# The heads' inverse root in the first mixer as exp of a logarithm on ScalarE, and two weight splits moved ahead of it

## The chip, the cores and the metric

One core of a Trainium2 chip runs the whole program in one launch. The metric is the device time of that launch in microseconds; lower is better. The engines are TensorE (PE, matrix products), VectorE (DVE), ScalarE (ACT), GpSimd (POOL) and SyncE (SP), which here only issues the loads of weights.

## What is computed

The reference runs two transformer blocks in float32 over 512 tokens of width 1024. The change lies in the first block's mixer:

```python
def l2_normalize(x):
    x32 = x.astype(jnp.float32)
    return x32 * lax.rsqrt(jnp.sum(x32 * x32, axis=-1, keepdims=True) + L2_EPS)

def hybrid_mixer(h, w_in, conv_qkv_w, ...):
    p = h @ w_in
    qkv = jax.nn.silu(causal_depthwise_conv(p[..., Q_OFF:Z_OFF], conv_qkv_w))
    q, k, v = ...                                   # 4 heads of 128 each
    o = gated_delta_rule_chunked(l2_normalize(q), l2_normalize(k), v, g, beta)
    ...
```

Four heads of k and four of q, each 128 x 512 (channels on partitions, tokens along the row), are divided by the root of their sum of squares plus 1e-6; q is also scaled by 128^-0.5. Behind the mixer come its output product, a feed-forward, and then the second block (feed-forward, a mixer with attention and a second recurrence, feed-forward, norm). None of that is touched.

## The kernel before

Everything is written out by hand: each engine has its own function (`tensor`, `vector`, `scalar`, `gpsimd`, `sync`), runs its instructions in the order in which they stand there, and waits on counting semaphores. `X.at(i)` is the point a waiter waits for, `X.up(i)` the increment.

**Weights.** They come as slabs of 128 x 1024 float32, one for each tile of 128 output columns. SyncE loads them into a ring of four buffers `RAWS` (L2270), strictly in the order of the list `ORDER`. In the stretch of the change that list alternates: a slab of `w_in`, then a slab of `ada`, and so on. A load waits until its buffer, used four entries earlier, has been read. For a `w_in` slab that means the split of the one two before it; for an `ada` slab, VectorE's weighing (`ada(j)`, L1024) of the one two before it. Each `w_in` slab is split into an upper part WH and a lower part WL, three buffers of each: ScalarE copies WH (L1625, `split_to`, reached through `begin(which, j, ahead)`), and GpSimd subtracts (L2087). A slab's WH waits for the product that used the same buffer three slabs earlier. The product itself (L490, `slab_gemm`) waits for WL and runs three passes over eight k tiles, 24 matmuls of 128 x 512.

**The mixer's first part.** `IN_ORDER` is the order of the `w_in` tiles: four heads of k, four of q, four of v (index i = 0 to 11), then four z tiles and twelve of the short convolution. I call the weights of index i "slab i" and its product "product i". The products write two PSUM banks in turn (`main_bank`), so product i waits until the result two places before it in the list `MAIN` has been copied out. `MAIN` has the `ada` column 2 between product 9 and product 10, so product 10 waits for tile 9, product 11 for VectorE's `modulation(2)` and product 12 for tile 10.

For each of the tiles 0 to 11, ScalarE's `convolve(i)` copies the product from PSUM to a staging buffer `STG` (L1702, `cv_ev`); VectorE's `convolve(i)` forms the causal convolution of width 4 with one TENSOR_SCALAR (L1106) and three SCALAR_TENSOR_TENSOR (L1109); ScalarE applies silu (L1704) and, for the eight tiles of k and q, squares the result into `L2S[i]` (L1707), which lies in `X`. In each turn i of its loop ScalarE first splits slab i + 1, and then calls `convolve(i - 1)`; VectorE first weighs an `ada` slab and then convolves. From i = 10 on, both go on in `project_rest`, a generator that is interleaved with the delta rule's generators by a fixed number of ticks.

**The heads' norm.** It runs in two batches of four tiles. TensorE sums the squares over the partitions with a matrix of ones (`l2_sums`, L554), after product 5 and after the `ada` column 2. ScalarE takes the roots from PSUM (`l2_roots`, L1712), in the turn i = 6 behind `convolve(5)`, and behind `convolve(9)`. VectorE divides (`unit_heads`): a RECIPROCAL (L1116) and one SCALAR_TENSOR_TENSOR (L1118) for each tile, in the turn i = 7 behind `convolve(6)`, and behind `convolve(9)` and `modulation(2)`.

**Function tables.** The compiler puts an ACT_TABLE_LOAD before a function that the loaded set does not have. `log_and_exp()` (L1632) is an explicit load of the set that has Ln and Exp; one also stands before `project_rest` starts, behind the second batch. Copy and Square cause no load in the profile.

The delta rule's `prepare` begins during product 13: TensorE (L662), then VectorE (L1255) and ScalarE (L1803), and waits for the end of the heads' norm.

Of the kernel before, what the change touches and what calls it, by code (L numbers as in the profile page):

```python
# [40 lines left out]
IN_ORDER = [4, 5, 6, 7, 0, 1, 2, 3] + list(range(8, 28))  # L41
# [105 lines left out]
def program(nc, xT, metaT, cols, consts, slabs, lup, gup, out):  # L147
    f32, f32r = mybir.dt.float32, mybir.dt.float32r
    ALU, ACT = mybir.AluOpType, mybir.ActivationFunctionType
    ve, ae, ge, te, se = nc.vector, nc.scalar, nc.gpsimd, nc.tensor, nc.sync  # L150
# [5 lines left out]
    def steps(name, *names):  # L156
        return Steps(sem(name), *names)

    def count(name):
        return Count(sem(name))  # L160
# [10 lines left out]
    def bank(i):  # L171
        return PS[:, i, :]
# [19 lines left out]
    EPSC = sbuf("EPSC", [128, 1])  # L192
# [144 lines left out]
    z_ev, sc_ev = count("z_ev"), count("sc_ev")  # L337
    sc = steps("sc", "prod", "t0", "t1", "t2", "y")
    cat1_hi, cat1_lo = count("cat1_hi"), count("cat1_lo")
    l2_sq, l2_mm, l2_rt = count("l2_sq"), count("l2_mm"), count("l2_rt")  # L340
    l2 = steps("l2", "rec", "mul")


    INV_PE = ("i1", "i2", "i3", "i4", "i5", "i6", "i7", "i8", "i9a", "i9b", "i10", "i11a", "i11b", "i12")
# [87 lines left out]
    L2S = [XF[:, 512 * i:512 * i + 512] for i in range(8)]  # L432
# [45 lines left out]
    def tensor():  # L478
# [70 lines left out]
        def l2_sums(i0):  # L549
            for i in range(i0, i0 + 4):  # L550
                if i in (4, 5):
                    te.wait_ge(*l2_rt.at(i - 2))
                te.wait_ge(*l2_sq.at(i))
                te.matmul(bank(i if i0 else 2 + i), con("ones"), L2S[i], start=True, stop=True).then_inc(*l2_mm.up(i))  # L554

# [93 lines left out]
        def prepare(b):  # L649
            e, t = b % 2, b // 2  # L650
            p, d, a = pp[e], dp[e], ap[e]
            A, B = bank(2 + 2 * e), bank(3 + 2 * e)
            ts = slice(128 * b, 128 * b + 128)
            te.wait_ge(s_k1, 32)
            te.wait_ge(*row_c.at("colt"))
            if t:
                te.wait_ge(*d.at("w2", t - 1))
                te.wait_ge(*a.at("w1", t - 1))
            else:
                te.wait_ge(*l2_rt.at(5 if e else 1))  # L660
            for h in range(4):
                ins = te.matmul(A[:, 128 * h:128 * h + 128], con("sel", 64)[:, 128 * h:128 * h + 128], ROW[:, ts],  # L662
                                start=True, stop=True)
            ins.then_inc(*p.up("g", t))
            for h in range(4):
                ins = te.matmul(B[:, 128 * h:128 * h + 128], con("sel", 64)[:, 128 * (4 + h):128 * (4 + h) + 128],
                                ROW[:, ts], start=True, stop=True)
            ins.then_inc(*p.up("bb", t))
            yield
            yield  # L670
            yield
            te.wait_ge(*a.at("eg", t))
            te.wait_ge(*l2.at("mul", 7))
            te.wait_ge(*d.at("kb", t))
            for h in range(4):
                for c, q in enumerate(HALF):
                    t0 = 64 * (2 * b + c)
                    te.matmul(A[q, 64 * h:64 * h + 64], QKV[:, 4 + h, t0:t0 + 64], KB[e][:, h, 64 * c:64 * c + 64],
                              start=True, stop=True)
                    ins = te.matmul(B[q, 64 * h:64 * h + 64], QKV[:, 4 + h, t0:t0 + 64], QKV[:, h, t0:t0 + 64],  # L680
                                    start=True, stop=True)
            ins.then_inc(*p.up("kq", t))
            yield
            te.wait_ge(*cv_si.at(11))
            te.wait_ge(*d.at("at", t))
            for h in range(4):
                te.transpose(A[:, 128 * h:128 * h + 128], QKV[:, 4 + h, ts], con("ident"))
                ins = te.transpose(B[:, 128 * h:128 * h + 128], QKV[:, 8 + h, ts], con("ident"))
            ins.then_inc(*p.up("tr", t))
            yield  # L690
            te.wait_ge(*d.at("vbt", t))
            yield from invert(inv[e], UU[e], p, d, a, gp[e], t, A, B)
            te.wait_ge(*d.at("x", t))
            for h in range(4):
                for q in HALF:
                    ins = te.matmul(A[q, 128 * h:128 * h + 128], XX[e][q, h, :], VBT[e][q, h, :], start=True, stop=True)
            ins.then_inc(*p.up("u", t))
            yield
            te.wait_ge(*a.at("u", t))
            for h in range(4):  # L700
                for q, o in zip(HALF, (B, A)):
                    ins = te.matmul(o[:, 64 * h:64 * h + 64], KBT[e][q, h, :], XX[e][q, h, :], start=True, stop=True)
            ins.then_inc(*p.up("w", t))

        def scan(b):
            e, t = b % 2, b // 2
            for c, q in enumerate(HALF):
                n = 2 * b + c
                te.wait_ge(*dp[e].at("w2", t))
                te.wait_ge(*ap[e].at("w1", t))  # L710
                if n:
                    te.wait_ge(*sd.at("st3", n - 1))
                    te.wait_ge(*so.at(n - 1))
                    if c == 0:
                        te.wait_ge(*gt_r.at("ln", b - 1))
                else:
                    te.wait_ge(*zeros.at("st"))
                    te.wait_ge(*l2_rt.at(7))
                for h in range(4):
                    ins = te.matmul(PS[q, 6, 128 * h:128 * h + 128], WT[e][:, 4 * c + h, :], ST[:, h, :], start=True,  # L720
                                    stop=True)
                ins.then_inc(*sp.up("s", n))
                yield
                te.wait_ge(*sd.at("vn", n))
                for h in range(4):
                    ins = te.matmul(PS[:, 7, 128 * h:128 * h + 128], KDT[e][q, h, :], VN[q, h, :], start=True, stop=True)
                ins.then_inc(*sp.up("sd", n))

                for h in range(4):
                    te.matmul(PS[:, 6, 64 * h:64 * h + 64], ST[:, h, :], QD[e][:, h, 64 * c:64 * c + 64], start=h == 0,  # L730
                              stop=False, skip_group_check=True)
                for h in range(4):
                    ins = te.matmul(PS[:, 6, 64 * h:64 * h + 64], VN[q, h, :], AT[e][q, h, :], start=False, stop=True,
                                    skip_group_check=True)
                ins.then_inc(*sp.up("o", n))
                yield
            te.wait_ge(*gt_sq.at(b))
            te.matmul(bank(6), con("ones"), RSTD[:, 0:512], start=True, stop=True).then_inc(*gt_mm.up(b))
            yield
            yield  # L740
# [272 lines left out]
    def vector():  # L1013
# [98 lines left out]
        def unit_heads(i0):  # L1112
            for i in range(i0, i0 + 4):
                j = IN_ORDER[i]
                ve.wait_ge(*l2_rt.at(i))
                ve.reciprocal(L2S[i], L2S[i]).then_inc(*l2.up("rec", i))  # L1116
                ve.wait_ge(*l2.at("rec", i))
                ve.scalar_tensor_tensor(QKV[:, j, :], QKV[:, j, :], 128.0 ** -0.5 if j < 4 else 1.0, L2S[i], ALU.mult,  # L1118
                                        ALU.mult).then_inc(*l2.up("mul", i))

        for i in range(1, 10):
            ada(i + 15)
# [118 lines left out]
        def prepare(b):  # L1241
            e, t = b % 2, b // 2
# [16 lines left out]
            ve.wait_ge(*d.at("dc1", t))  # L1259
            ve.tensor_tensor(dv, dv, over(con("madd"), 4), ALU.add).then_inc(*d.up("dm", t))  # L1260
            ve.wait_ge(*p.at("bb", t))
            ve.wait_ge(*l2.at("mul", 7))
            ve.tensor_tensor(KB[e][:, :, :], QKV[:, 4:8, ts], h4(B), ALU.mult).then_inc(*d.up("kb", t))
            ve.wait_ge(*a.at("eg", t))
            ve.tensor_tensor(QD[e][:, :, :], QKV[:, 0:4, ts], EG[e][:, :, :], ALU.mult).then_inc(*d.up("qd", t))
# [348 lines left out]
    def scalar():  # L1614
# [13 lines left out]
        def begin(which, j, ahead=2, cap=len(CUTS)):  # L1628
            split_to(min(CUT[which, j] + ahead, cap))

        def log_and_exp():
            ae.preload_act_table_set("natural_log_exp_and_others")  # L1632
# [74 lines left out]
                ae.activation(L2S[i], QKV[:, j, :], ACT.Square).then_inc(*l2_sq.up(i))  # L1707

        def l2_roots(i0):
            for i in range(i0, i0 + 4):  # L1710
                ae.wait_ge(*l2_mm.at(i))
                ae.activation(L2S[i], bank(i if i0 else 2 + i), ACT.Sqrt, bias=EPSC[:, 0:1]).then_inc(*l2_rt.up(i))  # L1712

        begin("w_in", IN_ORDER[0], 1)
        for i in range(1, 10):
# [14 lines left out]
            if i == 4:  # L1730
                ae.wait_ge(*row_c.at("colt"))
                ae.activation(EGC[:, :, :], COLT[:, :, 0:4], ACT.Exp).then_inc(*row_e.up(0))
            elif i == 6:
                l2_roots(0)
        begin("w_in", IN_ORDER[10], 1)
        convolve(9)
        l2_roots(4)

        def project_rest():
# [52 lines left out]
        def prepare(b):  # L1792
            e, t = b % 2, b // 2
# [5 lines left out]
            if t:  # L1799
                ae.wait_ge(*d.at("qd", t - 1))  # L1800
            else:
                ae.wait_ge(*l2.at("mul", 7))
            ae.activation(EG[e][:, :, :], h4(A), ACT.Exp).then_inc(*a.up("eg", t))  # L1803
            yield
            ae.wait_ge(*d.at("dm", t))
# [650 lines left out]
```

## Time and profile before

| | |
|---|---|
| time, median of 3 runs | 2199.66 us (2195.71 to 2201.82) |
| the profiled execution | 2196.09 us |
| its span, first to last instruction | 2194.9 us |
| PE busy | 1995.6 us, 91% |
| DVE busy | 823.5 us, 38% |
| POOL busy | 760.0 us, 35% |
| ACT busy | 701.4 us, 32% |
| mean granted TensorE clock | 0.957 of full |

The shares are means over the whole span. The change touches only about 75 us of it, from 110 to 185 us after the start, so that stretch has to be read by itself, in the order of time. A row of the timeline has the start, the time until the end of the last instruction of the row, the engine, the line, the operation, the output and inputs, and in brackets how long the engine had been idle before it, and what ended that.

### The profile page before, as it was taken

Reading aid. Unit: us, or ns where it says so; the run is one execution under the profiler, and the core shown is the slowest. Engines: PE = TensorE matmul, PEld = TensorE weight load, DVE = VectorE, ACT = ScalarE, POOL = GpSimd, SP = SyncE. Lnnn points to the kernel's source line nnn. Section 1 sums busy time; section 2 is a strip of 40 time slices with the busy share of each in tenths; the row PEclk is TensorE's granted clock in tenths of the full one; section 3 lists DMA queues with packets and bytes.
Section 4 is the critical chain, followed back from the end, with each engine's and each line's share of the span. In section 5 each row is a group of like instructions: output and inputs, shape, how many; then the busy total and the mean of one; then the engine's idle time right before and its main releaser. Section 6 shows DMA issues by size and latency. Waiting matters only on the chain. (4 is left out here: it accounts for less than half of the span.)

```text
span 2194.9 us, 32154 instructions
## 1 busy us (share of the span) xinstructions
PE 1995.6 (91%) x13960; PEld 1677.6 (76%) x13960; DVE 823.5 (38%) x1073; ACT 701.4 (32%) x1048; POOL 760.0 (35%) x444
## 2 busy tenths in 40 slices
PE   3866998899999999999999888888999789999997
PEld 2645776778888889999999877876676567888885
DVE  6677363332211112443400366654444433444201
ACT  2442221232222323222222333344454324222222
POOL 2312121334444555443344432211011144444453
PEclk9978999899999999999999999899998899999999
DMA  7322221223432232322323412100000232333331
GB/s 268 116 77 96 78 83 63 78 67 135 144 95 89 85 102 91 97 87 87 92 90 90 136 61 73 29 6 2 1 2 2 87 106 81 93 96 96 91 95 64
DMA packets 55659, 182.76 MB, mean 83 GB/s; under 512 B 7488, under 2 KB 7744, under 8 KB 55392
## 3 DMA queue, kind: packets, MB, share of 16 engines
q1 hardware_dynamic: 55520, 180.72, 25.6%
q8 instruction: 110, 1.80, 0.4%
q14 instruction: 29, 0.24, 0.0%
HBM read 175.45 MB, written 5.24 MB: 82 GB/s over the span
## 5 line engine op out<-in xcount | busy, mean ns | idle before, releaser
L2087 POOL TENSOR_TENSOR WL<-RAWS,WH 128x1024 fp32r<-128x1024 f32 (+2 forms) x275 | 647.7, 2358 | 1011.2 <-ACT WH L1625 1011.2
L490 PE MATMUL PS<-HH,WH 128*128 128x264 f32 (+2 forms) x2184 | 673.6, 350 | 58.5 <-issue 31.3
L490 PE MATMUL PS<-HL,WH 128*128 128x264 f32 (+2 forms) x2184 | 657.1, 343 | 0.0
L490 PE MATMUL PS<-HH,WL 128*128 128x264 f32 (+2 forms) x2184 | 654.5, 341 | 0.0
L490 PEld LDWEIGHTS PS<-HH,WH 128*128 128x128 f32 (+1 forms) x2184 | 381.0, 192 | 126.4 <-issue 55.9
L1625 ACT ACTIVATE WH<-RAWS 128x1024 fp32r<-128x1024 f32 (+2 forms) x275 | 283.8, 1033 | 452.7 <-PE PS L490 401.9
L490 PEld LDWEIGHTS PS<-HL,WH 128*128 128x128 f32 (+1 forms) x2184 | 381.2, 191 | 47.7 <-issue 1.9
L490 PEld LDWEIGHTS PS<-HH,WL 128*128 128x128 f32 (+1 forms) x2184 | 380.2, 191 | 48.5 <-issue 0.4
L490 PE MATMUL PS<-IHf,WH 128*128 128x512 f32 (+1 forms) x704 | 209.4, 338 | 0.0
L490 PE MATMUL PS<-IHf,WL 128*128 128x512 f32 (+1 forms) x704 | 209.3, 338 | 0.0
L490 PE MATMUL PS<-ILf,WH 128*128 128x512 f32 (+1 forms) x704 | 209.2, 338 | 0.0
L1372 DVE TENSOR_TENSOR TMP<-TMP,PS 128x512 f32<-128x512 f32 (+1 forms) x66 | 45.8, 693 | 250.9 <-PE PS L490 238.3
L1886 ACT ACTIVATE IHf<-TMP 128x512 fp32r<-128x512 f32 (+1 forms) x66 | 42.0, 636 | 283.4 <-DVE TMP L1372 283.4
L490 PEld LDWEIGHTS PS<-ILf,WH 128*128 128x128 f32 x704 | 120.6, 188 | 14.8
L490 PEld LDWEIGHTS PS<-IHf,WH 128*128 128x128 f32 x704 | 120.5, 188 | 14.8
L490 PEld LDWEIGHTS PS<-IHf,WL 128*128 128x128 f32 x704 | 120.4, 188 | 14.9
L1367 DVE TENSOR_TENSOR TMP<-TMP,RSTD 128x528 f32<-128x528 f32 (+1 forms) x44 | 104.5, 2374 | 41.4 <-ACT TMP L1882 41.4
L1379 DVE SCALAR_TENSOR_TENSOR X<-PS,X 128x528 f32<-128x528 f32 (+1 forms) x16 | 11.2, 699 | 222.5 <-PE PS L490 222.5
L1360 DVE TENSOR_TENSOR TMP<-PS,RSTD 128x528 f32<-128x528 f32 (+1 forms) x44 | 30.8, 700 | 150.9 <-PE PS L490 150.1
L2103 POOL TENSOR_TENSOR SQA<-SQA,TMP 128x512 f32<-128x512 f32 (+1 forms) x39 | 53.1, 1360 | 89.8 <-ACT TMP L1638 89.0
L1374 DVE TENSOR_TENSOR ILf<-TMP,IHf 128x512 fp32r<-128x512 f32 (+1 forms) x66 | 48.8, 740 | 46.4 <-ACT IHf L1886 46.4
L1638 ACT ACTIVATE TMP<-X 128x512 f32<-128x512 f32 (+1 forms) x42 | 26.1, 627 | 85.0 <-DVE X L1379 35.7
(494 smaller groups left out, 1948.8 us busy)
## 6 DMA issues: line engine op xcount, KB each, us to landing
RAWS<-w_w_in SPq DMA_DIRECT2D x52, 512.0 KB, 4.3
RAWS<-w_ada SPq DMA_DIRECT2D x32, 512.0 KB, 3.6
RAWS<-w_f0g SPq DMA_DIRECT2D x22, 512.0 KB, 3.6
RAWS<-w_f0u SPq DMA_DIRECT2D x22, 512.0 KB, 3.7
RAWS<-w_f1g SPq DMA_DIRECT2D x22, 512.0 KB, 3.6
RAWS<-w_f1u SPq DMA_DIRECT2D x22, 512.0 KB, 3.6
RAWS<-w_f2g SPq DMA_DIRECT2D x22, 512.0 KB, 3.6
RAWS<-w_f2u SPq DMA_DIRECT2D x22, 512.0 KB, 3.6
```

The costliest lines, as they stand in the source:

```text
L490: ins = te.matmul(ps[0:m, q, o:o + b - a] if len(halves) > 1 else ps[0:m, o:o + b - a], w[:, k * m:k * m + m], v[:, k0 + k, a:b], start=fi ...
L1360: ve.tensor_tensor(tv, place(f, 2 * j), r, ALU.mult).then_inc(*ff_g.up("g", FT * (f - 1) + j))
L1367: ve.tensor_tensor(tv, tv, r, ALU.mult).then_inc(*ff_g.up("r", FT * (f - 1) + j))
L1372: ve.tensor_tensor(tv, tv, place(f, 2 * j + 1), ALU.mult).then_inc(*ff_mul.up(FT * f + j))
L1374: ve.tensor_tensor(IL[f][:, j, :], t, IH[f][:, j, :].bitcast(f32), ALU.subtract).then_inc(*ff_lo.up(FT * f + j))
L1379: ve.scalar_tensor_tensor(xv, place(f, 2 * FT + m), 0.5 if f else MOD[:, 40 + m:41 + m], xv, ALU.mult, ALU.add).then_inc(*ff_x.up(8 * f + m))
L1625: ae.activation(WH[s % NS][:, 0:n], RAW[i % NR][:, 0:n], ACT.Copy).then_inc(*w_hi.up(s))
L1638: ae.activation((TMP[k % 3] if k else SQA)[:, 0:n], X[:, k, t0:T2], ACT.Square).then_inc(*n_sq.up(8 * SQUARED[q] + k))
L1886: ae.activation(IH[f][:, j, :], t, ACT.Copy).then_inc(*ff_hi.up(FT * f + j))
L2087: ge.tensor_tensor(WL[s % NS][:, 0:n], RAW[i % NR][:, 0:n], WH[s % NS][:, 0:n].bitcast(f32), ALU.subtract).then_inc(*w_lo.up(s))
L2103: ge.tensor_tensor(SQA[:, 0:n], SQA[:, 0:n], TMP[k % 3][:, 0:n], ALU.add).then_inc(*n_acc.up(added(q, k)[1] - 1))
```

## The change

`unit_heads` loses its RECIPROCAL: the SCALAR_TENSOR_TENSOR alone is left, and multiplies by what ScalarE hands over. `l2_roots` becomes a preload of the set with Ln and Exp, four times Ln (bias 1e-6) from PSUM, and four times Exp with scale -0.5 in place, in the place of four times Sqrt. TensorE's waits on `l2_rt`, which guard the PSUM banks, become waits on the new count `l2_ln`.

ScalarE also splits slab 8 before the first batch of roots (it was split behind it, ahead of `convolve(6)`), and slab 12 before the second batch (it was split behind `convolve(10)`'s silu, in `project_rest`). The later calls of `begin` for the same slabs then have nothing left to do. GpSimd's order and SyncE's are not changed.

```diff
@@ tensor()
-                    te.wait_ge(*l2_rt.at(i - 2))
+                    te.wait_ge(*l2_ln.at(i - 2))
@@ vector(), unit_heads
                 ve.wait_ge(*l2_rt.at(i))
-                ve.reciprocal(L2S[i], L2S[i]).then_inc(*l2.up("rec", i))
-                ve.wait_ge(*l2.at("rec", i))
                 ve.scalar_tensor_tensor(QKV[:, j, :], QKV[:, j, :], 128.0 ** -0.5 if j < 4 else 1.0, L2S[i], ALU.mult,
-                                        ALU.mult).then_inc(*l2.up("mul", i))
+                                        ALU.mult).then_inc(*l2.up(i))
@@ scalar()
         def l2_roots(i0):
+            log_and_exp()
             for i in range(i0, i0 + 4):
                 ae.wait_ge(*l2_mm.at(i))
-                ae.activation(L2S[i], bank(i if i0 else 2 + i), ACT.Sqrt, bias=EPSC[:, 0:1]).then_inc(*l2_rt.up(i))
+                ae.activation(L2S[i], bank(i if i0 else 2 + i), ACT.Ln, bias=EPSC[:, 0:1]).then_inc(*l2_ln.up(i))
+            for i in range(i0, i0 + 4):
+                ae.wait_ge(*l2_ln.at(i))
+                ae.activation(L2S[i], L2S[i], ACT.Exp, scale=-0.5).then_inc(*l2_rt.up(i))
@@
             elif i == 6:
+                begin("w_in", IN_ORDER[7], 1)
                 l2_roots(0)
         begin("w_in", IN_ORDER[10], 1)
         convolve(9)
+        begin("w_in", IN_ORDER[11], 1)
         l2_roots(4)
```

## Rows read from the trace of the kernel before

**Rows 1.** What TensorE waited for, 100 to 192 us (total, times, longest).

```profile
PE PS L490 <- issue: 24.2, 3, 17.6
PE PS L525 <- ACT STG L1702: 14.1, 1, 14.1
```

**Rows 2.** Timeline of ScalarE, the first batch and around it.

```profile
103.25 0.63 ACT L1707 ACTIVATE X<-QKV 128x512 f32<-128x512 f32 x1
103.79 1.05 ACT L1625 ACTIVATE WH<-RAWS 128x1024 fp32r<-128x1024 f32 x1
...
110.62 0.63 ACT L1707 ACTIVATE X<-QKV 128x512 f32<-128x512 f32 x1
111.27 1.28 ACT L1712 ACT_TABLE_LOAD   x1
112.57 2.42 ACT L1712 ACTIVATE X<-PS,EPSC 128x512 f32<-128x512 f32 x4
114.86 1.07 ACT L1625 ACTIVATE WH<-RAWS 128x1024 fp32r<-128x1024 f32 x1
115.81 0.61 ACT L1702 ACTIVATE STG<-PS 128x512 f32<-128x512 f32 x1
```

**Rows 3.** Timeline of ScalarE: explicit loads, Ln and Exp in the delta rule and later.

```profile
238.72 1.28 ACT L1632 ACT_TABLE_LOAD   x1
...
458.32 1.28 ACT L1632 ACT_TABLE_LOAD   x1
459.62 0.69 ACT L1653 ACTIVATE RSTD<-PS,EPSC 128x512 f32<-128x512 f32 x1
460.34 0.63 ACT L1655 ACTIVATE RSTD<-RSTD 128x512 f32<-128x512 f32 x1
```

**Rows 4.** Timeline of VectorE, 68 to 140 us.

```profile
68.75 0.49 DVE L1106 TENSOR_SCALAR TMP<-STG,CV 128x512 f32<-128x512 f32 x1
69.28 2.33 DVE L1109 SCALAR_TENSOR_TENSOR TMP<-STG,CV,TMP 128x512 f32<-128x512 f32 x3
71.52 1.28 DVE L1024 SCALAR_TENSOR_TENSOR ACC<-RAWS,CA,ACC 128x1024 f32<-128x1024 f32 x1
...
116.45 2.18 DVE L1106 TENSOR_SCALAR TMP<-STG,CV 128x512 f32<-128x512 f32 x1 [5.33 <-ACT STG L1702]
...
120.91 3.34 DVE L1116 RECIPROCAL X<-X 128x512 f32<-128x512 f32 x1
...
138.18 1.28 DVE L1024 SCALAR_TENSOR_TENSOR ACC<-RAWS,CA,ACC 128x1024 f32<-128x1024 f32 x1
```

**Rows 5.** VectorE's multiply by its line (duration in ns, min/median/max).

```profile
L1118 DVE SCALAR_TENSOR_TENSOR QKV<-QKV,X x8: 691/694/2003, 124.3 to 175.4; 128x512 f32<-128x512 f32 x8
```

**Rows 6.** Timeline of GpSimd: the split of slab 8.

```profile
116.01 2.34 POOL L2087 TENSOR_TENSOR WL<-RAWS,WH 128x1024 fp32r<-128x1024 f32 x1 [8.73 <-ACT WH L1625]
```

**Rows 7.** Timeline of SyncE's queue: the load of slab 10.

```profile
139.86 0.43 SPq L2270 DMA_DIRECT2D RAWS<-w_w_in  x1
```

**Rows 8.** Timeline of ScalarE, between the batches and behind the second.

```profile
144.50 1.06 ACT L1625 ACTIVATE WH<-RAWS 128x1024 fp32r<-128x1024 f32 x1 [0.96 <-DMA RAWS<-w_w_in]
...
157.33 0.63 ACT L1704 ACTIVATE QKV<-TMP 128x512 f32<-128x512 f32 x1 [4.62 <-DVE TMP L1109]
...
180.03 0.63 ACT L1704 ACTIVATE QKV<-TMP 128x512 f32<-128x512 f32 x1 [15.12 <-DVE TMP L1109]
```

**Rows 9.** Timeline of TensorE: the first matmuls of products 12 and 13.

```profile
184.13 0.76 PE L490 MATMUL PS<-HH,WH 128*128 128x512 f32 x1 [17.61 <-issue]
184.69 0.63 PE L490 MATMUL PS<-HL,WH 128*128 128x512 f32 x1
...
191.54 0.40 PE L490 MATMUL PS<-HH,WH 128*128 128x512 f32 x1
```

**Rows 10.** Windows: busy time of PE, PEld, DVE, ACT and POOL, then TensorE's clock.

```profile
112.00:184.00 72.00, 35.14 (x126) 25.84 (x124) 59.06 (x43) 22.80 (x31) 11.74 (x5) 0.74 0.23 79
460.00:850.00 390.00, 386.49 (x1704) 313.63 (x1705) 69.67 (x93) 120.24 (x155) 178.71 (x83) 0.99 0.32 101
```

More of the change, by code:

```diff
@@ L339, in program @@
     cat1_hi, cat1_lo = count("cat1_hi"), count("cat1_lo")
-    l2_sq, l2_mm, l2_rt = count("l2_sq"), count("l2_mm"), count("l2_rt")
-    l2 = steps("l2", "rec", "mul")
+    l2_sq, l2_mm, l2_ln, l2_rt, l2 = (count(x) for x in ("l2_sq", "l2_mm", "l2_ln", "l2_rt", "l2"))
     INV_PE = ("i1", "i2", "i3", "i4", "i5", "i6", "i7", "i8", "i9a", "i9b", "i10", "i11a", "i11b", "i12")
@@ L659, in prepare @@
             else:
-                te.wait_ge(*l2_rt.at(5 if e else 1))
+                te.wait_ge(*l2_ln.at(5 if e else 1))
             for h in range(4):
@@ L672, in prepare @@
             te.wait_ge(*a.at("eg", t))
-            te.wait_ge(*l2.at("mul", 7))
+            te.wait_ge(*l2.at(7))
             te.wait_ge(*d.at("kb", t))
@@ L717, in scan @@
                     te.wait_ge(*zeros.at("st"))
-                    te.wait_ge(*l2_rt.at(7))
+                    te.wait_ge(*l2_ln.at(7))
                 for h in range(4):
@@ L1261, in prepare @@
             ve.wait_ge(*p.at("bb", t))
-            ve.wait_ge(*l2.at("mul", 7))
+            ve.wait_ge(*l2.at(7))
             ve.tensor_tensor(KB[e][:, :, :], QKV[:, 4:8, ts], h4(B), ALU.mult).then_inc(*d.up("kb", t))
@@ L1801, in prepare @@
             else:
-                ae.wait_ge(*l2.at("mul", 7))
+                ae.wait_ge(*l2.at(7))
             ae.activation(EG[e][:, :, :], h4(A), ACT.Exp).then_inc(*a.up("eg", t))
```

## The prediction

> **What bounds the kernel now.** I first read what TensorE waited for, because the change sits in a short stretch and the shares over the whole span say nothing of it. From 100 to 192 us TensorE waits 24.2 us in three pieces put down to "issue" (the longest 17.6) and 14.1 us for a copy to STG [rows 1]. Those 38.3 us of idle time are all that can be won here. Then I read the timelines of ScalarE and VectorE beside each other. In the first batch ScalarE's roots take 3.6 us, and VectorE then spends 17.27 us from the first RECIPROCAL at 120.91 to the next `ada` at 138.18 [rows 2, 4], in pairs of 3.34 and 0.69 us [rows 4, 5]. Everything behind that is held up in turn: silu(7), the split of slab 10, the copy of tile 8 right behind it, for which TensorE waits 14.1 us [rows 1, 8]. In the second batch, silu(9) starts at 157.33 and silu(10) only at 180.03, after 15.12 us of waiting for VectorE [rows 8]; slab 12 is split behind it, and product 12 starts at 184.13 after 17.61 us of idleness [rows 9]. So the bound in this stretch is the chain from VectorE over ScalarE's silu and split to GpSimd's WL, and TensorE is the waiting engine. In 112 to 184 us it is busy 35.14 of 72 us, against 386.49 of 390 in the first feed-forward [rows 10].
>
> **The sum, first batch.** All times are in the profiled execution; nothing changes before ScalarE's square at 110.62 [rows 2].
> - Split of slab 8, moved ahead: an instruction behind a 0.63 us activation starts 0.54 us after it (103.25 to 103.79), so the split runs from 111.16 to 112.23 [rows 2]. Its buffer was loaded and its WH buffer is free, as product 6 is done. GpSimd has WL at about 115.7 in place of 118.35 [rows 6].
> - Load, Ln, Exp: the load starts at 112.23 and the first Ln 1.30 us later [rows 3], at 113.53. I cost four Ln as the four Sqrt, which have the same operands and length (0.69 us), 2.29 us [rows 2, 3]: 115.82. Four Exp from SBUF take 0.63 us each [rows 3], 0.54 us apart: 117.98. If they went at Ln's pace it would be 0.15 us more for a batch. The copy of tile 6 thus starts at 117.98 in place of 115.81, 2.17 us later. Product 8 then waits for this copy (118.6) instead of for WL (118.35): 0.2 us.
> - VectorE's convolution of tile 6 starts at 118.62. GpSimd is idle by then, and TENSOR_SCALAR takes 0.53 us to the next start, as at 68.75, and not 2.18, as at 116.45 beside GpSimd's split [rows 4, 6]. With three SCALAR_TENSOR_TENSOR at 2.24 us together it ends at 121.39, against 120.91. The moved split so pays back most of ScalarE's 2.17 us.
> - The norm on VectorE: four multiplies at 0.69 us each, about 0.61 us apart: 2.44 us in place of 17.27. It ends at 123.83, against 138.18.
> - Next, ScalarE: silu(6) 121.5, square 122.2, split of slab 9 from 122.7, and GpSimd 1.15 us after it (114.86 to 116.01) [rows 2, 6], at 123.86. That is a dead heat with `ada(23)` on VectorE at 123.83. If GpSimd is first, `ada(23)` ends at about 127.1 and the convolution of tile 7 at 129.9. If VectorE is first, `ada(23)` ends at 125.1, GpSimd at 127.5, the TENSOR_SCALAR is held until then, and the convolution ends at 130.0. A multiply of 2.00 us among seven of 0.69 shows this kind of hold on VectorE [rows 5].
> - Slab 10: its load is queued on SyncE behind an `ada` load that waits for `ada(23)`. Before, `ada(23)` ended at 139.46, the load was issued at 139.86, and the split began at 144.50, 5.04 us after `ada(23)` [rows 4, 7, 8]. Now that gives 130.15 or 132.15, and ScalarE is ready at 131.2. The split begins at 131.2 or 132.15: 13.3 or 12.35 us earlier. I take 12.8.
>
> The Trainium skill (SBUF — State Buffer, section "SBUF: two separate sides") states the port shared by VectorE and GpSimd as an exclusive lock: whichever starts first has it for its whole instruction. The row of 2.00 us agrees for GpSimd first; the other case has no row here. By that rule alone either end of the last step is possible, so it speaks for 12.35 as much as for 13.3.
>
> **The sum, second batch.** From slab 10 to silu(9) nothing is changed: 144.50 to 157.33 becomes 131.7 to 144.5 [rows 8]. The split of slab 12 follows at 145.05 (its load waits for `ada(25)`, at about 139, and so lands at about 144), the table load at 146.1, Ln at 147.4, Exp at 149.7. The sums of squares are ready well before. VectorE multiplies from 150.35, each Exp just ahead of it, until 152.8; `ada(26)` to 154.0. ScalarE has one more explicit load, the one that stands ahead of `project_rest`. Though redundant now, it is issued: the row at 458.32 is such a load, and no other set was loaded since the one at 238.72 [rows 3]. So the copy of tile 10 runs from 153.15 to 153.75, hidden behind `ada(26)`; without that cover the 1.3 us would be on the chain. The convolution of tile 10, with no GpSimd beside it, ends at 156.8, and silu(10) starts at 156.9 in place of 180.03: 23.1 us earlier. Then come `ada(27)` and the convolution of tile 11, again unhindered, to 160.85, silu(11) at 160.95, the split of slab 13 at 161.5, and GpSimd from 162.65 to 165.0. Product 12 has its weights long before (slab 12 is moved ahead) and runs at about 154 to 160, right behind product 11. **Product 13** starts at 165.05 in place of 191.54: 26.5 us earlier. But now it is the cold one, after 5 us of idleness. Product 12 took 7.41 us for 24 matmuls after its gap, with 0.76 and 0.63 us rows where later ones have 0.40 [rows 9]; in the feed-forward one comes every 0.229 us, 5.5 us for 24 [rows 10]. So 1.9 us go back. What remains is 26.5 - 1.9 = **24.6 us**. What is late next is the pair of silu(11) and split 13, and from product 13 on TensorE itself. TensorE's idle time checks it: 38.3 us before; after, 5.4 ahead of product 8, about 2 ahead of product 9, 1 and 5 ahead of product 13, some 13 in all, 25 less.
>
> Removed waits hide nothing else: TensorE's waits move to `l2_ln`, which comes at the time of the old roots. Later stages are driven by semaphores only, with loads in a ring, so they shift as they are.
>
> **The time.** 2196.09 - 24.6 = 2171.5 us for the profiled execution. It lies 3.6 us under the median of the runs shown, while the mean of all four executions is 2198.3. From that, 2173.7; I say 2174.
>
> **The rivals.**
> - *The forecast*, 24.6 us, chance 0.70.
> - *A table load between Ln and Exp*, if the two were not in the loaded set: 1.3 us for each batch on the chain, 2.6 in all, 2176.6. Against it: Exp follows Ln at 460.34 without one [rows 3]. It is also the case that the change does not do quite what it says. 0.05.
> - *The weight ring takes over.* The work is packed closer, and slabs 10 and 12 each arrive later than 5.04 us after their `ada`. If each took twice that, 4 to 5 us a batch are lost: about 15.5 us won, 2183. For it: split 10 already waited 0.96 us for its load [rows 8]. Against it: the loads share of the DMA engines is only 0.23 here [rows 10]. 0.09.
> - *More than forecast*: VectorE first in the dead heat and no cold start: 24.6 + 0.5 + 1.9 = 27.0, 2171; and if the delta rule's start closes up too, up to 5 us more. 0.08, half of it in the range.
> - *No change*, if a wait elsewhere in the stage took all: 2198. Rows 1 and 9 speak against it, since TensorE waits for exactly this chain. 0.05.
> - *Slower*: the granted clock of the long product stages falls because TensorE comes to them with less rest. They run at 0.99 [rows 10]. About 1155 us of them would have to fall by 24.6/1155 = 2.1%, to 0.97, to decide it; at 0.96 (3%, 35 us) the time would be 2174 + 35 = 2209. No row shows rest being paid back; the clock is low only around gaps, 0.74 against 0.99 [rows 10]. 0.03.
>
> **How the numbers follow.** The bounds of the terms give 21.5 to 27.0 us won, 2171.3 to 2176.8 on the mean; the executions before spread from 2195.71 to 2201.82, three either way. The range is 2167 to 2181, with 0.79 in it. About 0.3%, 6.6 us, is what a measurement of this kernel can tell from no change. Faster by more than that: 0.92; within: 0.05; slower: 0.03.
>
> **What would show it.** In the profile after: no RECIPROCAL in this stretch; VectorE's batches of about 2.4 us; a TENSOR_SCALAR of 0.49 us for tile 6; split 10 at 131 to 132; silu(10) near 157; product 12 directly behind product 11; product 13 near 165 and cold; two more loads at L1632, those at L1712 gone; and the stages behind shifted by one constant. If the shift shrinks or grows from stage to stage, or split 10 is later than 133, the prediction is wrong at that step.

## The result, and the profile after

| | before | after |
|---|---|---|
| time, median | 2197.68 us (2194.95 to 2201.82, 4 runs) | 2176.48 us (2170.92 to 2179.63, 4 runs) |
| the profiled execution | 2196.09 us | 2179.63 us |
| its span | 2194.9 us | 2178.4 us |
| mean granted TensorE clock | 0.957 | 0.954 |

The ratio after/before is 0.9898, 95% interval 0.9883 to 0.9914. On 2197.68 us that is 22.4 us less (18.9 to 25.7); the two medians differ by 21.2 us. The forecast was 24.6 us, and 2174 us.

The two profiled executions differ by 16.5 us, less than the runs do. So spans alone would mislead here, and I read the profile by distances inside the stretch. Three marks serve: **silu(5)**, the last ScalarE instruction ahead of the change that both kernels share (it starts at 109.96 before and 110.48 after, the start of the program differs by up to 1.3 us from execution to execution); **product 13**, its first matmul; and **the second pair**, the second time that the delta rule's selection matmuls (L662 before, L661 after) start, when product 13 has run four of its eight k tiles.

First what TensorE waited for between 100 and 168 us in the profile after (total, times, longest), which answers to [rows 1]:

```profile
PE PS L489 <- ACT STG L1699: 8.9, 3, 5.3
PE PS L489 <- issue: 6.4, 3, 3.8
```

Of 38.3 us of idle time 15.3 are left (8.9 + 6.4). Now the timeline of ScalarE after, first batch, beside [rows 2]:

```profile
110.48 0.63 ACT L1701 ACTIVATE QKV<-TMP 128x512 f32<-128x512 f32 x1 [4.64 <-DVE TMP L1108]
111.15 0.63 ACT L1704 ACTIVATE X<-QKV 128x512 f32<-128x512 f32 x1
111.69 1.04 ACT L1622 ACTIVATE WH<-RAWS 128x1024 fp32r<-128x1024 f32 x1
112.75 1.28 ACT L1629 ACT_TABLE_LOAD   x1
114.05 2.42 ACT L1710 ACTIVATE X<-PS,EPSC 128x512 f32<-128x512 f32 x4
116.34 2.20 ACT L1713 ACTIVATE X<-X 128x512 f32<-128x512 f32 x4
118.42 0.60 ACT L1699 ACTIVATE STG<-PS 128x512 f32<-128x512 f32 x1
```

and of VectorE, then GpSimd, beside [rows 4] and [rows 6]:

```profile
119.06 0.48 DVE L1105 TENSOR_SCALAR TMP<-STG,CV 128x512 f32<-128x512 f32 x1 [7.41 <-ACT STG L1699]
...
121.82 2.49 DVE L1115 SCALAR_TENSOR_TENSOR QKV<-QKV,X 128x512 f32<-128x512 f32 x4
124.23 1.28 DVE L1023 SCALAR_TENSOR_TENSOR ACC<-RAWS,CA,ACC 128x1024 f32<-128x1024 f32 x1
125.42 2.60 DVE L1105 TENSOR_SCALAR TMP<-STG,CV 128x512 f32<-128x512 f32 x1
```

```profile
124.26 3.48 POOL L2090 TENSOR_TENSOR WL<-RAWS,WH 128x1024 fp32r<-128x1024 f32 x1 [9.09 <-ACT WH L1622]
```

The norm holds VectorE 2.41 us (121.82 to 124.23) where it held it 17.27 [rows 4]. The reader also sees the dead heat of the forecast: VectorE's `ada(23)` started 0.03 us ahead of GpSimd, GpSimd's row is stretched to 3.48 us from 2.34, and the TENSOR_SCALAR behind it to 2.60 from 0.48.

Last, TensorE after, the first matmuls of products 12 and 13, and the selection matmuls, beside [rows 9]:

```profile
153.89 0.80 PE L489 MATMUL PS<-HH,WH 128*128 128x512 f32 x1 [2.52 <-ACT STG L1699]
...
165.03 0.76 PE L489 MATMUL PS<-HH,WH 128*128 128x512 f32 x1 [3.82 <-issue]
...
167.85 2.07 PE L661 MATMUL PS<-ROW,KC 64*128 64x128 f32 x8
...
174.34 1.16 PE L661 MATMUL PS<-ROW,KC 64*128 64x128 f32 x8
```

and the same pair in the kernel before:

```profile
193.03 1.16 PE L662 MATMUL PS<-ROW,KC 64*128 64x128 f32 x8
...
196.59 1.16 PE L662 MATMUL PS<-ROW,KC 64*128 64x128 f32 x8
```

Product 13 starts 54.55 us behind silu(5); the forecast had 55.09 (165.05 - 109.96). But TensorE is cold there until the second pair. Cold means that the granted clock is 0.50 of full, the lower of its two levels (1.2 and 2.4 GHz), as it was from 167 to 174 us. A matmul of 128 x 512 then has a row of 0.63 us instead of 0.40. Eight selection matmuls take 2.07 us instead of 1.16, and the two pairs lie 6.49 us apart instead of 3.56. (A pair is the eight matmuls of L661, shown, and the eight of L665 behind them.) The second pair comes 63.86 us behind silu(5), against 86.63 before: 22.8 us of lead.

### The profile page after: what moved, and what is told of

Read it like the earlier page. It is cut to its first block and busy times, and to the rows that moved or that the text cites. A ratio compares the mean times of both kernels' runs of the same rounds, so it can differ in the third digit from the quotient of the medians.

```text
span 2178.4 us, 32154 instructions
## 1 busy us (share of the span) xinstructions
PE 2005.8 (92%) x13960; PEld 1688.1 (77%) x13960; DVE 789.1 (36%) x1065; ACT 706.8 (32%) x1056; POOL 762.8 (35%) x444
## 5 line engine op out<-in xcount | busy, mean ns | idle before, releaser
L1635 ACT ACTIVATE TMP<-X 128x512 f32<-128x512 f32 (+1 forms) x42 | 26.2, 628 | 84.8 <-DVE X L1376 35.7
```

The lines of the kernel that those rows point to most:

```text
L1635: ae.activation((TMP[k % 3] if k else SQA)[:, 0:n], X[:, k, t0:T2], ACT.Square).then_inc(*n_sq.up(8 * SQUARED[q] + k))
```

## The experiments

Three questions stood after the result. Does the lead come from the chain over VectorE, and what is each part of the change worth (E1 to E3)? Is the gap ahead of product 13 what the low clock costs (E4 to E6)? And why is the difference of the two profiled spans smaller than the lead in the stretch (E9, E10)? E7 tests whether the redundant table load is hidden, and E8 puts to use what the others showed. Theory A: the chain of splits alone sets the time. Its rival, theory B: once TensorE rests, its cold start takes back what an earlier split of one slab gives.

**E1, the norm alone**, without the two moved splits:

```diff
             elif i == 6:
-                begin("w_in", IN_ORDER[7], 1)
                 l2_roots(0)
...
-        begin("w_in", IN_ORDER[11], 1)
         l2_roots(4)
```

> The change without its two moved splits: slab 8 is split behind the first batch of roots and slab 12 behind silu(10), as before. By the theory that the chain of splits sets the time (theory A), WL of slab 13 and the start of product 13 come about 4 us later than in the changed kernel (165.0 to about 169), and so does everything behind. By the theory that TensorE's cold start takes the place of its wait (theory B), product 12 now starts cold at about 161.5, and product 13 follows it directly and at the full clock, so the second pair of the delta rule's first matmuls (L661) starts near 174, as in the changed kernel (174.34), and the time is the same within 1 us: 2176 by B, 2180 by A.

Measured: median 2176.75 us over 4 runs, ratio to before 0.9897 (0.9882 to 0.9911). The timeline of TensorE:

```profile
161.64 0.77 PE L489 MATMUL PS<-HH,WH 128*128 128x512 f32 x1 [8.66 <-issue]
...
169.03 0.40 PE L489 MATMUL PS<-HH,WH 128*128 128x512 f32 x1
...
170.51 1.16 PE L661 MATMUL PS<-ROW,KC 64*128 64x128 f32 x8
...
174.08 1.16 PE L661 MATMUL PS<-ROW,KC 64*128 64x128 f32 x8
```

Product 12 has WL of slab 12 late and starts cold, after 8.66 us of waiting. But product 13 (169.03) then follows without a gap, and the selection matmuls are at the full clock (1.16 us). The first pair comes 60.08 us behind silu(5), 2.7 us later than in the changed kernel (57.37); the second 63.65, which is 0.2 us earlier. That is theory B, which had the second pair near 174, and the time at 2176; theory A had 2180.

**E2, the two moved splits alone**, with Sqrt and RECIPROCAL as before:

```diff
             elif i == 6:
+                begin("w_in", IN_ORDER[7], 1)
                 l2_roots(0)
...
+        begin("w_in", IN_ORDER[11], 1)
         l2_roots(4)
```

> Only the two moved splits, with the old Sqrt and RECIPROCAL. Theory A: WL of slab 13 at about 187.4 in place of 190.8, product 13 at 187.4 in place of 191.5, so 3 to 4 us faster than before. Theory B: product 12 runs early, at about 165 to 170, TensorE then rests 17 us, product 13 is cold for some 9 us, and the second pair of L662 starts within 1 us of before (196.6): no gain.

Measured: 2196.31 us over 10 runs, ratio 0.9988 (0.9978 to 0.9998), which is 2.6 us less. The timeline of TensorE:

```profile
188.41 0.77 PE L490 MATMUL PS<-HH,WH 128*128 128x512 f32 x1 [17.64 <-issue]
...
191.24 2.07 PE L662 MATMUL PS<-ROW,KC 64*128 64x128 f32 x8
...
197.81 2.07 PE L662 MATMUL PS<-ROW,KC 64*128 64x128 f32 x8
```

Product 13, 77.34 us behind silu(5), is 4.2 us ahead of before (191.54 - 109.96 = 81.58), as expected. The second pair is at 86.74, against 86.63 before: all of it given back, and that pair too is still cold (2.07); in this execution the granted clock stays at 0.50 until 206.4. GpSimd even starts on slab 15 at 208.45, 97.38 us behind silu(5), against 95.67 before. The interval, 0.4 to 4.8 us less, holds theory A's gain and nearly none at all, so the times do not decide; this one profile speaks for B. Where the 2.6 us of the runs come from is not shown. An execution with a shorter cold start, as E5 below has one, would keep part of the 4.2 us, but no such execution of this kernel was profiled; and single executions differ by more for other reasons (E9, below).

**E3, without the moved split of slab 12 only:**

```diff
-        begin("w_in", IN_ORDER[11], 1)
         l2_roots(4)
```

> The change without the second moved split (slab 12 behind silu(10) as before); the one of slab 8 stays. Theory A: product 13 starts at about 167.4 in place of 165.0, and the time is 2.4 us longer than the changed kernel's. Theory B: product 12 is the cold one (from about 160), product 13 follows warm, the second pair of L661 starts at about 172.4 in place of 174.3, and the time is 2 us shorter than the changed kernel's.

Measured: 2174.08 us over 4 runs, ratio 0.9880 (0.9863 to 0.9896). Product 12 starts cold at 160.40 after 8.69 us, the two pairs at 169.83 and 173.40; silu(5) is at 110.86. So the second pair comes at 62.54, 1.3 us before that of the changed kernel's profile (and 1.6 us behind that of E5, below). Product 13 starts 2.9 us later than in the changed kernel (57.48 us behind silu(5) against 54.55), but warm. So the moved split of slab 12, which looks like 2.9 us on the chain, is worth nothing that the runs can tell: 2174.08 without it, 2176.48 with it, and the intervals overlap.

**E4, the gap ahead of product 13 filled:**

```diff
         def project_rest():
             for i in range(10, 28):
+                if i == 13:
+                    te.wait_ge(*l2_ln.at(7))
+                    for x in range(16):
+                        te.matmul(bank(6), HH[:, 0, NM:NM + 128], HL[:, 0, NM:T2], start=True, stop=True)
                 yield from project(IN_ORDER[i])
```

> The changed kernel with 16 matmuls of 128 x 512 between products 12 and 13, into a PSUM bank that is free then; their result is not used. They take about 3.8 us of the idle time (160.8 to 165.0) and delay nothing. If the idle time ahead of product 13 is what makes it cold, product 13 starts at 165.0 at the full clock, its first six matmuls and the two pairs of L661 take 1.4 + 2 x 2 us as before the change, the second pair starts at about 170.0 in place of 174.3, and the time is 4 us shorter. If the low clock comes from the whole stretch before (idle or cold for 50 us), the filling changes it by less than 1 us.

Measured: 2173.97 us over 4 runs, ratio 0.9884 (0.9869 to 0.9899), an interval that overlaps the changed kernel's, so the times do not show the gain. The timeline of TensorE:

```profile
165.71 0.47 PE L489 MATMUL PS<-HH,WH 128*128 128x512 f32 x1
...
167.26 1.16 PE L665 MATMUL PS<-ROW,KC 64*128 64x128 f32 x8
...
170.82 1.16 PE L665 MATMUL PS<-ROW,KC 64*128 64x128 f32 x8
```

Product 13 starts where it did, 54.57 us behind silu(5) (111.14), but warm, and the second pair comes at 59.68, 4.2 us earlier than in the changed kernel's profile. In that profile, however, product 12's first matmul also took only 0.50 us, after the same wait of 2.52 us after which it took 0.80 in the changed kernel (the low clock came four matmuls later). So the clock at product 13 could have been chance, and both were repeated.

**E5 and E6, the changed kernel and the filled one once more** (no edit).

> The changed kernel itself once more, as a control for the clock. Counted from silu(5): if the gap ahead of product 13 makes it cold, product 13 is cold again (rows of 0.63 us into the first L661 pair), and the second pair of L661 starts 63.9 us after silu(5), within 0.5. If its clock was chance in that one execution, it starts anywhere between 59.7 and 64.

> The changed kernel with 16 matmuls in the gap ahead of product 13 once more. By the filling, the second pair of L661 starts 59.7 us after silu(5) again, 4.2 us earlier than without. If it was chance: near 63.9 at least at times.

TensorE in E5, the changed kernel:

```profile
164.40 0.76 PE L489 MATMUL PS<-HH,WH 128*128 128x512 f32 x1 [3.73 <-issue]
...
167.23 1.20 PE L661 MATMUL PS<-ROW,KC 64*128 64x128 f32 x8
...
170.84 1.16 PE L661 MATMUL PS<-ROW,KC 64*128 64x128 f32 x8
```

Of the two readings of E5 the first, 63.9 us again, failed, and the second, that the clock differs from one execution to the next, held. Product 13 is cold again after its gap, but only for its first six matmuls, and the second pair comes at 60.97, not 63.86. The filled kernel gives 59.72 again. What the gap costs is therefore 1.3 us in one execution and 4.2 in another. The Trainium skill (TensorE: Matmul & The Clock Gate, "Part 1: The HAM clock gate") states that the same kernel measures different numbers of cold matmuls from run to run. These traces agree: six cold matmuls of 128 x 512 at product 13 in E5, twelve and a cold pair in the changed kernel's first profile.

**E7, without the redundant table load** ahead of `project_rest`:

```diff
-        log_and_exp()
         alternate(pr, pr, dr, dr, pr, pr, dr, dr, dr)
```

> The changed kernel without the redundant explicit table load ahead of project_rest. By my cover, the copy of tile 10 ends 1.3 us earlier, but VectorE's ada(26) ends where it did, so silu(10) stays 46.4 us after silu(5), and product 13 at 54.55. If the load is on the chain, both come 1.3 us earlier.

Measured (one execution, 2173.88 us): tile 10 is copied from 152.35, right behind Exp; silu(5) starts at 111.04 and silu(10) at 157.44, so 46.40 us, and product 13 at 165.57, 54.53. The cover holds to 0.02 us. The second pair is at 61.18. Product 12 starts 1.4 us earlier and stays warm here, so the gap ahead of product 13 is longer, 6.72 us, and yet the cold start costs only 1.5 us.

**E8, the idle stretches put to use.** The core of the edit; every instruction of the changed kernel is still there but the redundant load:

```diff
@@ vector()
         for i in range(1, 10):
-            ada(i + 15)
+            if i != 8:
+                ada(i + 15)
+            if i == 7:
+                ada(23)
...
         modulation(2, bank(MAIN_AT["ada", 2] % 2))
+        ada(26)
+        convolve(10)
         unit_heads(4)
@@ scalar(), where copy_out(i) is the copy from PSUM that convolve(i) begins with
                 begin("w_in", IN_ORDER[7], 1)
+                copy_out(6)
                 l2_roots(0)
...
         begin("w_in", IN_ORDER[11], 1)
+        copy_out(10)
         l2_roots(4)
...
                 if i < 12:
-                    convolve(i)
+                    if i == 11:
+                        begin("w_in", IN_ORDER[12], 1)
+                    convolve(i, i == 10)
                     continue
...
-        log_and_exp()
         alternate(pr, pr, dr, dr, pr, pr, dr, dr, dr)
```

> The changed kernel with its idle stretches put to use, nothing left out: ScalarE copies tile 6 and tile 10 from PSUM before it takes the roots, not behind them, so that VectorE convolves beside the roots; VectorE weighs ada(23) and ada(26) and convolves tile 10 in its idle time ahead of each norm batch; slab 13 is split right behind silu(10); the redundant load is gone. If the chain over VectorE, ScalarE's splits and GpSimd sets the time: silu(10) comes 5.9 us earlier (near 151), WL of slab 13 is ready at about 155 in place of 165, product 13 follows product 12 nearly at once and at the full clock, the second pair of L661 starts near 160 in place of 174, and the time is 12 to 14 us under the changed kernel's: about 2163. If the weight loads were the next bound, slab 10 or 13 would wait for its load and half of that at most would come.

Measured: 2163.96 us over 5 runs (2161.99 to 2169.27), ratio to before 0.9850 (0.9836 to 0.9863): 12.5 us under the changed kernel's median, 10.6 by the two ratios, and the fastest kernel of the study. First TensorE's waits from 100 to 160 us, then its timeline at product 13:

```profile
PE PS L489 <- issue: 7.6, 4, 3.9
```

```profile
156.39 0.47 PE L489 MATMUL PS<-HH,WH 128*128 128x512 f32 x1 [0.72 <-issue]
...
157.96 1.16 PE L661 MATMUL PS<-ROW,KC 64*128 64x128 f32 x8
...
161.53 1.16 PE L661 MATMUL PS<-ROW,KC 64*128 64x128 f32 x8
```

Product 13 waits 0.72 us and is warm; silu(5) is at 110.56, so the second pair comes at 50.97, 10.0 to 13.0 us before the changed kernel's in its three profiles. Both theories take part: the chain is shorter, and the cold start is gone with the gap. I had silu(10) 1.3 us too early (152.25 against 151), because the table load for silu, at 150.95, now stands on the chain. No split waited for a weight load. What each of the moved pieces brings is not separated.

**E9 and E10, before and changed kernel once more** (only a comment added).

> The kernel before once more. Question: in the changed kernel's two profiles the lead of 22 to 26 us at slab 15 shrinks by 5 us between slabs 22 and 33, at a lower granted clock; in the profile of before that stretch (300 to 430 us) has few low windows. If the low clock there is a matter of the single execution, this profile of before may show it too, and slab 33 then comes up to 5 us later after slab 15 than in the first profile of before (223.3 us), or not at all. If the change causes it, before shows 223.3 again, within 0.5.

> The changed kernel a third time, for the same question. If the low clock between slabs 22 and 33 is a matter of the single execution, the distance from slab 15 to slab 33 differs from the 228.2 and 228.3 us of its first two profiles, by up to 5 us downwards. If the change causes it, it is 228 again. And for the start of product 13: the second pair of L661 is 60.9 to 63.9 us behind silu(5), never under 60.5 if the gap ahead of it is what costs.

The distance from GpSimd's split of slab 15 to that of slab 33, through the delta rule. First the two splits of the profile of before, then those of E9, the same kernel:

```profile
205.63 2.38 POOL L2087 TENSOR_TENSOR WL<-RAWS,WH 128x1024 fp32r<-128x1024 f32 x1 [9.92 <-ACT WH L1625]
...
428.91 2.41 POOL L2087 TENSOR_TENSOR WL<-RAWS,WH 128x1024 fp32r<-128x1024 f32 x1
```

```profile
205.92 2.38 POOL L2087 TENSOR_TENSOR WL<-RAWS,WH 128x1024 fp32r<-128x1024 f32 x1 [9.90 <-ACT WH L1625]
...
435.65 2.42 POOL L2087 TENSOR_TENSOR WL<-RAWS,WH 128x1024 fp32r<-128x1024 f32 x1
```

It is 223.28 us in one execution of the kernel before and 229.73 in the other. The windows of that stretch (PE, PEld, DVE, ACT, POOL busy, then TensorE's clock, DMA share, GB/s), before, E9 and the changed kernel:

```profile
205.63:428.91 223.28, 203.73 (x1850) 160.58 (x1849) 96.23 (x178) 55.18 (x94) 47.83 (x26) 0.95 0.22 72
```

```profile
205.92:435.65 229.73, 211.05 (x1850) 166.50 (x1849) 96.76 (x178) 55.17 (x94) 47.75 (x26) 0.92 0.21 70
```

```profile
183.39:411.58 228.19, 209.48 (x1850) 165.53 (x1849) 96.83 (x178) 55.28 (x94) 47.85 (x27) 0.93 0.21 71
```

The same 1850 matmuls take 203.73 us at a clock of 0.95, 211.05 at 0.92 and 209.48 at 0.93; the busy time of VectorE, ScalarE and GpSimd differs by 0.6 us at most. The three profiles of the changed kernel have 228.2, 228.3 and 228.8 us, E1 has 223.2 with the same code in this stretch, and 203.73 us for the matmuls at 0.95, exactly as before. The other six profiles have 223.9 (E3), 225.2 (E2), 225.4 (E7), 225.6 (E8), 227.1 (E4) and 229.7 (E6, the same kernel as E4). So the 5 us that the changed kernel's profiled execution loses there are a matter of the clock in that execution, not of the change's instructions. Whether the change makes such an execution more frequent is open: all three profiles of the changed kernel are among the slower ones, one of the two of before as well, and that is too few to tell.

E10 also gives the start of product 13 a third time: cold through the first pair (2.07 us), the second pair at 63.94.

All marks in one table (us behind silu(5); worked out from the timelines; the times were taken beside runs of the kernel before with a median of 2199.38 us for E1 to E4 and 2198.83 for E8, so small differences between rows go by the ratios given above):

| kernel | first pair | second pair | lead of the second over 86.63 | time |
|---|---|---|---|---|
| before, and E9 | 83.07, 82.70 | 86.63, 86.27 | 0, 0.4 | 2197.68 |
| changed, and E5, E10 | 57.37, 57.36, 57.37 | 63.86, 60.97, 63.94 | 22.8, 25.7, 22.7 | 2176.48 |
| E1, norm alone | 60.08 | 63.65 | 23.0 | 2176.75 |
| E2, splits alone | 80.17 | 86.74 | -0.1 | 2196.31 |
| E3, slab 12 not moved | 58.97 | 62.54 | 24.1 | 2174.08 |
| E4, E6, gap filled | 56.12, 56.16 | 59.68, 59.72 | 27.0, 26.9 | 2173.97 |
| E7, a load less | 57.37 | 61.18 | 25.5 | one execution |
| E8, reordered | 47.40 | 50.97 | 35.7 | 2163.96 |

## Why the prediction was right, and where it was not

- **The bound.** Right: the time was in the waits of TensorE on the chain from VectorE. E1 takes only the norm and has the whole gain (0.9897 against 0.9898).
- **ScalarE's block.** The copy of tile 6 starts 7.94 us behind silu(5), forecast 8.02. Ln goes at Sqrt's pace, Exp at 0.52 to 0.53 us.
- **The norm on VectorE.** 2.41 us, forecast 2.44.
- **The dead heat.** VectorE was first, in the changed kernel's profile and with a row of 3.48 or 3.49 us in E1 and E3 too. The rule of the exclusive port that the forecast cites from the Trainium skill (SBUF — State Buffer, section "SBUF: two separate sides") had no row then for VectorE first; now the row of 3.48 us agrees. silu(7) came at 19.94 us behind silu(5), where both cases had given about 20.0. The load of slab 10 was then early enough, and the split came 13.4 us earlier than before; I had taken the mean of the two cases, 12.8. That is, to 0.1 us, the 0.5 us by which silu(10) (46.40, forecast 46.94) and product 13 (54.55, forecast 55.09) were early.
- **Product 12** does not run right behind product 11, as I wrote: product 11 was done by 151.4, since TensorE's earlier work was warm, and product 12 waits 2.52 us for the copy of tile 10. It costs nothing, since product 13 waits for slab 13 anyway.
- **The cold start** is the mis-sized term. I took 1.9 us from product 12 of the kernel before. Against the filled kernel (59.7) it cost 4.2, 1.3 and 4.2 us in three executions of the same kernel, and 1.5 in E7, 2.8 on the mean of the four. In the longer cases the clock stays low over both groups of the first pair, in 2.07 and 1.91 us rows, which I had not counted. The lead at the second pair is 22.8, 25.7 and 22.7 us, mean 23.7, against 24.6 forecast. That the two lie so close is in part luck: product 13's early start and the longer cold start have opposite signs.
- **The moved splits** were costed as part of the sum, and I let them pay back ScalarE's extra work. By product 13 they do (54.55 us behind silu(5) in the changed kernel, 58.60 in E1, 4.05 us earlier). By the second pair they are worth nothing in the first profiles (-0.1 us in E2 against before, -0.2 in the changed kernel against E1) and at most 2.7 in the best execution (63.65 in E1 against 60.97 in E5). So theory B holds wholly in some executions and in part in others. The step of the forecast that failed is this one: I read their worth at the start of product 13, and not behind the cold start that they bring.
- **The redundant load.** Issued, 1.28 us, and hidden, by E7 to 0.02 us.
- **The stages behind** shift as they are, but for the clock of the single execution. E1's lead over before, from split to split of GpSimd, is 22.5 us at slab 15, 22.8 from 600 to 1200 us and 22.1 from 1780 us to the end. The range of 2167 to 2181 had 3 us either way for this, and the changed kernel's runs spread over 8.7 us.
- **The rivals.** None decided. The slower one, a lower clock in the product stages, is in part what happened between slabs 15 and 33, but for 5 us only, and in one execution of the kernel before as well; the mean clock went from 0.957 to 0.954.

## What to carry to other kernels

Cost a step by where the work behind it runs at the full clock again, not by where its first user starts: an earlier product that leaves TensorE resting ahead of the next one only moves the cold start. Look for the cheapest gain in the idle rows that a change leaves behind: here copying out two tiles ahead of the roots and weighing two slabs in idle time (with one tile convolved and one more slab split early) brought 12.5 us by the medians on top of the 21 of the change itself, with nothing removed but one load. And compare kernels by distances between marks in the trace, with a second profile of each, before a difference of a few microseconds is put down to anything.

## What the runs showed of the hardware

- GpSimd can be the one that waits for VectorE: its split had a row of 3.48 us instead of 2.34 to 2.41 when VectorE's instruction with two SBUF inputs had started 0.03 us earlier, and VectorE's next one was held in turn, 2.60 us instead of 0.48. The waiting shows as a longer row, not as idle time.
- The clock can fall some time after a wait is over. After a wait of 2.5 us, product 12's first matmul took 0.80 us in one execution of the changed kernel, 0.69 in another (E10) and 0.50 in E4, E5 and E6. But in those three the low clock came one to four matmuls later: seven or eight of the 24 matmuls were slow (rows of 0.54 us and more) in each of the five, and from the first start to the last the product took 6.9 to 7.0 us. In E7, after a wait of 1.10 us, none was slow, and it took 5.4.
- A longer wait did not mean a longer cold start. After waits of 3.7 to 3.8 us, TensorE stayed cold for 2.8 us in one execution and for about 9 us in two others; after 6.72 us (E7) for about 3; after 17.6 to 17.8 us for 3.9 in before, 3.5 in E9 and 18 in E2, where from 188.4 to 206.4 TensorE was busy 17.99 of 18.00 us at a granted clock of 0.50.
- An explicit table load is carried out even when its set is already loaded: 1.28 us.
